# Two fused transformer blocks on one core: products of a constant tile between attention jobs and before norm turns, turns in blocks, new begin times

## The reference

```python
# first block, for each of 2 layers
h = h + 0.5 * swiglu(rmsnorm(h, ffn1_norm[l]), ...)            # 1024 -> 2816 -> 1024
z = rmsnorm(h, mix_norm[l]) @ w_in[l]                          # MLA, differential attention, pooling
...
h = h + merged @ w_out[l]
h = h + 0.5 * swiglu(rmsnorm(h, ffn2_norm[l]), ...)
# after the layers: rmsnorm(h, final_norm)

# second block, for each of 2 layers
x = x + 0.5 * rms_norm(swiglu_2(rms_norm(x, ...), ...), ...)
mix = token_mixing(rms_norm(x, ...), ...)     # windowed GQA with sinks, chunked mLSTM, RWKV-7 scan
x = x + rms_norm(mix, ln_mix_post[l])
x = x + 0.5 * rms_norm(swiglu_2(rms_norm(x, ...), ...), ...)
gate = jax.nn.sigmoid(rms_norm(x, ln_ple_pre[l]) @ w_ple_gate[l])
x = x + rms_norm(gate * (p[l] @ w_ple_proj[l]), ln_ple_post[l])
```

## Time and profile before

| | us |
|---|---|
| median of three runs | 2437.96 |
| lowest, highest | 2436.68, 2438.85 |
| the profiled execution | 2437.84 |
| its span, first to last instruction | 2436.5 |
| PE busy in it | 2380.6 |
| mean granted clock of TensorE | 0.982 |

### The profile page before, as it was taken

One profiled execution on the slowest core, in us unless ns is written; L12 is line 12 of the kernel. 1 busy time (PEld: TensorE's weight loads), 2 busy tenths in 40 slices (PEclk: granted clock), 3 DMA queues, 4 the chain that ended last, 5 costly groups with the idle time before them and its releaser, 6 DMA issues.

```text
span 2436.5 us, 31092 instructions
## 1 busy us (share of the span) xinstructions
PE 2380.6 (98%) x12448; PEld 1932.5 (79%) x12448; DVE 1520.9 (62%) x2296; ACT 1241.0 (51%) x2057; POOL 51.5 (2%) x66
## 2 busy tenths in 40 slices
PE   8999999999999999999999999999999999999998
PEld 6788878888888877888878878778877887877886
DVE  5656786655655778665565576665556558576555
ACT  5455554544544655454454463654455446365445
POOL 0000000000000000000000000000000000000000
PEclk9999999999999999999999999799999999979999
DMA  7555446555555434555555542155545553215563
GB/s 249 183 193 161 122 139 193 182 187 182 182 183 197 151 124 145 185 182 193 187 173 181 192 137 81 47 186 195 189 156 184 188 183 120 89 66 185 181 198 118
DMA packets 110737, 399.95 MB, mean 164 GB/s; under 512 B 12288, under 2 KB 12672, under 8 KB 110336
## 3 DMA queue, kind: packets, MB, share of 16 engines
q1 hardware_dynamic: 110592, 397.96, 49.9%
HBM read 396.86 MB, written 1.05 MB: 163 GB/s over the span
## 4 chain that ended last, share of the span: by engine, by line
PE 92%; DVE 4%; ACT 2%; issue 0%; POOL 0%; DMA 0%; SPq 0%; ACTq 0%
PE ps L489 81%; PE ps L498 4%; DVE wlo L478 1%; PE ps L2050 1%; PE ps L1456 1%; DVE alo L632 1%; PE ps L1420 1%; PE ps L2424 1%; ACT whi L471 0%; ACT ahi L613 0%; PE ps L1411 0%; PE ps L2553 0%; DVE xs L893 0%; PE ps L2542 0%; PE ps L2534 0%
## 5 line engine op out<-in xcount | busy, mean ns | idle before, releaser
L478 DVE TENSOR_TENSOR wlo<-raw,whi 128x1024 fp32r<-128x1024 f32 (+1 forms) x748 | 893.5, 1212 | 250.8 <-ACT whi L471 245.5
L471 ACT CAST whi<-raw 128x1024 fp32r<-128x1024 f32 (+1 forms) x748 | 764.1, 1041 | 295.1 <-PE ps L489 286.2
L489 PE MATMUL ps<-whi,ahi 128*128 128x512 f32 (+2 forms) x2016 | 812.3, 403 | 24.8 <-DVE wlo L478 18.2
L489 PE MATMUL ps<-wlo,ahi 128*128 128x512 f32 (+2 forms) x2016 | 809.4, 401 | 0.0
L489 PE MATMUL ps<-whi,alo 128*128 128x512 f32 (+2 forms) x2016 | 804.5, 399 | 0.0
L489 PEld LDWEIGHTS ps<-whi,ahi 128*128 128x128 f32 x2016 | 380.6, 189 | 124.2 <-DVE wlo L478 32.3
L489 PEld LDWEIGHTS ps<-wlo,ahi 128*128 128x128 f32 x2016 | 381.3, 189 | 82.9 <-issue 1.0
L489 PEld LDWEIGHTS ps<-whi,alo 128*128 128x128 f32 x2016 | 380.8, 189 | 81.1 <-issue 1.4
L489 PE MATMUL ps<-whi,yhi 128*128 128x512 f32 (+1 forms) x948 | 375.6, 396 | 0.5
L489 PE MATMUL ps<-wlo,yhi 128*128 128x512 f32 (+1 forms) x948 | 372.5, 393 | 0.0
L489 PE MATMUL ps<-whi,ylo 128*128 128x512 f32 (+1 forms) x948 | 372.1, 392 | 0.0
(11 more groups left out here) (374 smaller groups left out, 1627.6 us busy)
## 6 DMA issues: line engine op xcount, KB each, us to landing
raw<-stream SPq DMA_DIRECT2D x718, 512.0 KB, 4.1
raw<-stream SPq DMA_DIRECT2D x16, 388.0 KB, 3.1
bcb<-bcs SPq DMA_DIRECT2D x9, 512.0 KB, 4.6
raw<-stream SPq DMA_DIRECT2D x8, 416.0 KB, 3.8
raw<-stream SPq DMA_DIRECT2D x4, 384.0 KB, 3.0
cst<-consts SPq DMA_DIRECT2D x1, 1260.0 KB, 8.1
msc<-misc SPq DMA_DIRECT2D x1, 1160.0 KB, 6.9
xs<-xin SPq DMA_DIRECT2D x2, 512.0 KB, 4.5
```

Source lines behind the costliest of these rows:

```text
L471: act.do.copy(whi[:, n % NSP, 0:w], raw[:, n % NRAW, 0:w]).then_inc(*rounded(n))
L478: dve.do.tensor_tensor(wlo[:, n % NSP, 0:w], raw[:, n % NRAW, 0:w], whi[:, n % NSP, 0:w].bitcast(F), ALU.subtract).then_inc(*rest(n))
L489: m = pe.do.matmul(o, a, b, start=(first and q == 0), stop=(last and q == n - 1))
```

## The change

There are three edits.

First, a new constant tile `warm` (128x128, a copy of the identity in fp32r that DVE makes once) and a helper `rewarm`. It issues on PE as many products as a table `WARM` says for this boundary, lane and step. Each has `warm` as weights and `warm` four times over as 512 columns, is written to a bank that the next step overwrites, and is read by nobody. They stand before the norm turns (`pe_norm`), before scores of jobs (`pe_scores2`, bank 5) and before turns of jobs (`pe_values2`, bank 7). Each of these steps is now split in two: the wait for the bank and the products, then the wait for the data and the work. In `pe_values2` the wait for the copy of the job before stands ahead of the products and the wait for the exponentials behind them. In all there are 77 products: 24 in the jobs of mix2 and 3 in the norm before it, in each of two layers (54), and 23 in other norms.

Second, `turns` is no generator any more: its turns are issued in a row.

Third, every begin time of `PLAN` is new.

```diff
+WARM = {
+    "ffn1_2>mix2": {"pe_norm": (0, 0, 3, 0), "pe_scores2": (0, 0, 0, 0, 0, 2, 0, 5), "pe_values2": (0, 0, 0, 0, 6, 3, 3, 5)},
+    "ffn2>ffn1": {"pe_norm": (0, 0, 2, 0)},
+    "ffn2_2>ple": {"pe_norm": (0, 0, 0, 2)},
+    "final>ffn1_2": {"pe_norm": (0, 3, 3, 0)},
+    "mix2>ffn2_2": {"pe_norm": (0, 0, 0, 1)},
+    "ple>ffn1_2": {"pe_norm": (3, 6, 0, 0)},
+}
...
-        "act_project2": (28.12, 42.6, 53.34, 57.6, 65.86, 80.76, 99.02, 106.66, 111.42, 113.18, 148.8, 152.98),
...
+        "act_project2": (32.16, 37.1, 44.86, 59.1, 67.46, 88.24, 97.82, 103.12, 126.8, 127.96, 146.34, 148.84),
...
+    def rewarm(s, lane, n, bank):
+
+        counts = WARM.get(boundary(s), {}).get(lane, ())
+        for _ in range(counts[n] if n < len(counts) else 0):
+            pe.wait_ge(warm_dve, "made")
+            pe.do.matmul(ps[:, bank, :].rearrange("p (k n) -> p k n", k=4), warm[:, :],
+                         warm[:, :].unsqueeze(1).broadcast_to([128, 4, 128]), start=True, stop=True)
...
-    def turns(t, *each):
-
-        for q, (o, src) in enumerate(each):
-            if q:
-                yield (t + MM * q,)
+    def turns(*each):
+
+        for o, src in each:
             m = pe.do.transpose(o, src, ident)
         return m
...
     def pe_norm(s):
         for i in range(2):
             for hf in range(2):
+                yield turn_time(s, i, hf) - 0.01
+                wait_banks(s, i, hf)
+                rewarm(s, "pe_norm", 2 * i + hf, 2 * i + hf)
                 yield turn_time(s, i, hf)
                 wait_x(pe, s, i, hf)
-                wait_banks(s, i, hf)
...
             dve.wait_ge(load_tab, "pos")
+            if q == 0:
+                dve.do.tensor_copy(warm[:, :], ident).then_inc(*warm_dve("made"))
...
     def pe_scores2(s):
         for n, i, j, t in JOBS2:
-            yield org(s) + 20 + t
+            yield org(s) + 20 + t - 0.01
             k = 128 * (i + 1)
             if n:
                 pe.wait_ge(job_dve, s, n - 1, "mask")
             else:
                 pe.wait_ge(front_act, s, "qT")
                 pe.wait_ge(front_dve, s, "qT", 2)
+            rewarm(s, "pe_scores2", n, 5)
+            yield org(s) + 20 + t
...
     def pe_values2(s):
         for n, i, j, t in JOBS2:
-            yield org(s) + 20 + t + 3.0
+            yield org(s) + 20 + t + 2.99
             k = 128 * (i + 1)
-            pe.wait_ge(job_act, s, n, "exp", 1)
             if n:
                 pe.wait_ge(job_act, s, n - 1, "back")
             else:
                 pe.wait_ge(lstm_dve, s, "mq")
+            rewarm(s, "pe_values2", n, 7)
+            yield org(s) + 20 + t + 3.0
+            pe.wait_ge(job_act, s, n, "exp", 1)
```

More of the change, by code:

```diff
@@ new lines @@
+        "act_latent": (33.58, 34.74, 35.8, 39.26, 39.32, 39.32, 42.82, 49.6, 50.06, 54.44, 55.08, 55.08, 55.08),
+        "act_merged1": (196.34, 200.14, 204.8, 218.18),
+        "act_norm": (18.48, 22.16, 27.8, 28.24),
+        "act_pool1": (115.8, 116.14, 119.48, 132.32),
+        "act_project1": (52.08, 66.06, 85.16, 100.36),
+        "act_square": (17.04, 21.9, 28.32, 28.32),
+        "act_sums1": (151.84, 186.38),
+        "act_turn1": (116.74, 116.74, 190.48, 190.64),
+        "act_turns1": (67.1, 83.14, 100.84),
@@ new lines @@
+        "dve_square": (24.34, 33.08),
+        "dve_state": (131.26, 137.9, 139.52),
+        "dve_sums2": (149.52, 151.34, 172.2, 172.94),
+        "dve_turn2": (173.56, 174.3),
+        "dve_unit0": (55.66, 56.06, 71.02, 84.6, 89.94, 94.94, 108.74, 118.1),
+        "dve_unit1": (67.46, 79.88, 80.6, 86.16, 93.82, 101.66, 124.94, 132.82),
+        "pe_front2": (38.18, 38.8, 42.52, 54.1, 55.84),
+        "pe_group": (138.8, 142.94),
+        "pe_memory": (138.8, 147.52, 154.3, 159.02, 162.74, 168.98, 171.42, 171.42, 172.48, 174.5, 177.7, 178.04,
+            182.76),
@@ L297 @@
[L297 removed]
+        "act_post": (8.86, 9.02, 11.66, 19.76),
+        "dve_post": (5.28, 6.14, 11.66, 16.02, 16.76, 16.76),
+        "pool_post": (7.92, 15.2),
     },
     "ple>ffn1_2": {
[L300 to L305 removed]
@@ L309 @@
+        "pool_post": (-18.08, -0.38),
     },
@@ L377, in program @@
     rope2 = place("rope2", [2, 32])
+    warm = place("warm", [128], R)
     scr = spot[0]
@@ L572, in turn_time, with boundary @@
         return x_ready(s, i, hf) + (1.0 if i and hf else 0.3)
+    def boundary(s):
+        return (PARTS[s - 1][0] if s else "") + ">" + (PARTS[s][0] if s < len(PARTS) else "")
     def timed(s, **lanes):
-        key = (PARTS[s - 1][0] if s else "") + ">" + (PARTS[s][0] if s < len(PARTS) else "")
+        key = boundary(s)
         def one(name, lane):
@@ L773, in pe_hidden @@
                 pe.wait_ge(a_lo, s, 1, 7)
-            m = yield from turns(0, *((ps[:, 3, 256 * k + 128 * i:256 * k + 128 * i + 128],
+            m = turns(*((ps[:, 3, 256 * k + 128 * i:256 * k + 128 * i + 128],
                                        hid[:, (2 * q + i) % 4, 128 * k:128 * k + 128]) for k in range(2) for i in range(2)))
@@ L976, in pe_turn @@
     def pe_turn(sig, s, name, o, bank, b):
-        m = yield from turns(0, *((ps[:, bank, 256 * c + 128 * i:256 * c + 128 * i + 128],
+        m = turns(*((ps[:, bank, 256 * c + 128 * i:256 * c + 128 * i + 128],
                                    o[:, i, 256 * b + 128 * c:256 * b + 128 * c + 128]) for c in range(2) for i in range(2)))
@@ L1034, in pe_chunks @@
                 yield (4 * MM,)
-            m = yield from turns(4 * MM * b, *((ps[:, banks[b], 256 * c + 128 * i:256 * c + 128 * i + 128],
+            m = turns(*((ps[:, banks[b], 256 * c + 128 * i:256 * c + 128 * i + 128],
                                                   src(i)[:, 256 * b + 128 * c:256 * b + 128 * c + 128])
@@ L1202, in pe_latent @@
             pe.wait_ge(front_dve, s, "cn", 1, g)
-            m = yield from turns(4 * MM * g, *((ps[:, 2 + g, 256 * (c % 2) + 128 * i:256 * (c % 2) + 128 * i + 128],
+            m = turns(*((ps[:, 2 + g, 256 * (c % 2) + 128 * i:256 * (c % 2) + 128 * i + 128],
                                                   cn[:, i, 128 * c:128 * c + 128]) for c in cs for i in range(2)))
@@ L1248, in pe_latent @@
                 pe.wait_ge(front_dve, s, "v", 0)
-            m = yield from turns(0, *((ps[0:96, QT_BANKS[b], 256 * (h % 2) + 128 * i:256 * (h % 2) + 128 * i + 128],
+            m = turns(*((ps[0:96, QT_BANKS[b], 256 * (h % 2) + 128 * i:256 * (h % 2) + 128 * i + 128],
                                        qs[:, i, h, :]) for h in ((2 * b, 2 * b + 1) if b < 4 else (8,)) for i in range(2)))
@@ L1437, in pe_values1 @@
                 pe.wait_ge(job_dve, s, n, "mix")
-            m = yield from turns(0, *((ps[:, 7, 128 * j:128 * j + 128], a[:, 128 * j:128 * j + 128])
+            m = turns(*((ps[:, 7, 128 * j:128 * j + 128], a[:, 128 * j:128 * j + 128])
                                       for j in range(2 * (i + 1) if kind == "mla" else i + 1)))
@@ L1588, in pe_turn1 @@
                     pe.wait_ge(*back_turn1(s, 7))
-                yield from pe_turn(job_pe, s, kind, o, bank[b], b)
+                pe_turn(job_pe, s, kind, o, bank[b], b)
     def act_turn1(s, l):
@@ L2384, in pe_rope2 @@
             pe.wait_ge(rec_dve, s, 1, "T")
-            m = yield from turns(0, *((ps[:, 4 + b, 256 * (c % 2) + 128 * i:256 * (c % 2) + 128 * i + 128],
+            m = turns(*((ps[:, 4 + b, 256 * (c % 2) + 128 * i:256 * (c % 2) + 128 * i + 128],
                                        qk2[:, i, 2 * c:2 * c + 2, :].rearrange("p h d -> p (h d)"))
@@ L2413, in pe_values2 @@
                 pe.wait_ge(lstm_dve, s, "mq")
-            m = yield from turns(0, *((ps[:, 7, 128 * q:128 * q + 128], S2[:, n % 2, 128 * q:128 * q + 128])
+            rewarm(s, "pe_values2", n, 7)
+            yield org(s) + 20 + t + 3.0
+            pe.wait_ge(job_act, s, n, "exp", 1)
+            m = turns(*((ps[:, 7, 128 * q:128 * q + 128], S2[:, n % 2, 128 * q:128 * q + 128])
                                       for q in range(2 * (i + 1))))
@@ L2489, in pe_turn2 @@
             pe.wait_ge(job_dve, s, "out", 1)
-            yield from pe_turn(job_pe, s, "att", o_att, 5 + b, b)
+            pe_turn(job_pe, s, "att", o_att, 5 + b, b)
     def act_turn2(s):
@@ L2556, in pe_memory @@
         pe.wait_ge(lstm_dve, s, "out", 1)
-        yield from pe_turn(lstm_pe, s, "mem", hm, 0, 0)
+        pe_turn(lstm_pe, s, "mem", hm, 0, 0)
     def act_memory(s, l):
```

270 lines of the change are left out of this document (125 added, 145 removed), and 61 rows, old and new, of the table PLAN.

## The result

| | before | after |
|---|---|---|
| median of four runs, us | 2438.40 | 2410.51 |
| lowest, highest | 2436.68, 2439.02 | 2409.24, 2412.00 |
| the profiled execution | 2437.84 | 2412.00 |
| its span | 2436.5 | 2410.7 |
| PE busy | 2380.6 | 2363.4 |

The changed kernel takes 0.9887 of the time, 95% interval 0.987 to 0.9904: 27.9 us less, where 16.7 were forecast. The page after, beside the earlier trace rows: busy us of each engine, and the clock in 40 slices.

A forecast was written before the change was run, and what follows sets the result against it. PE, busy 98% of the span, was taken as the bound, with 55.9 us idle and 82 us at half clock. 15.0 + 3.0 - 2.3 + 1.0 = 16.7 us faster gave 2421 us; range 2403 to 2440.

The forecast's parts named there:

- New begin times: Order on all queues at every stage boundary: taken as 0, with 8 us each way in the range.
- Rival two: PE's 25 us of boundary waits for `wlo` and `xs` shrink by half, 12 us: 2409 us, chance 0.11.
- Long stretches: Half-clock pieces late in both mix2 stages run at full clock: 22.3 us gross, 15.0 us net of hops and products.
- DVE-bound piece: Mix2 piece where DVE is nearly full: a quicker PE gains 0, at most 4.6 and 5.6 us in the two layers.
- Rival three: All 82 us at half clock count, DVE-bound pieces shorten too: 41 us less products, 2401 us, chance 0.06.
- The price of the products: 0.23 us each; 19 of 24 in each layer's jobs hidden, the 5 ahead of job 7's turns cost 1.15 us.
- table loads: ACT saves two loads of 1.28 us per mix2 layer: 1 us faster for both layers, between 0 and 5.1.
- short stretches: Brief half-clock windows of 3.4 to 6.8 us: 3 us faster, between 0 and 7.2.
- products elsewhere: Of 29 products outside the jobs, 10 are charged in full: 2.3 us slower, ends 0 and 6.7.
- Rival one: The clock falls later in the jobs but still falls, half of 22.3 us is lost: 2431 us, chance 0.20.
- Rival four: The clock falls where it did, just ahead of 1547 us, and later products only burden PE: 2454 us, chance 0.10.
- Rival five: Long stretches gain, but new begin times add 16 us of waits for `wlo`: 2437 us, chance 0.08.

The follow-up runs named there:

- no_products: The changed kernel without any of its 77 `warm` products, new begin times and turns in a row kept: 2434.08 us, ratio 0.9983.
- old_begin_times: The changed kernel with every begin time of the kernel before, products and turns in a row kept: 2426.95 us, ratio 0.996.
- more_norm: The changed kernel with 17 more products in norms (mix2's norm and final>ffn1_2): 2410.51 us, ratio 0.9891.
- jobs_early: The changed kernel without the last 11 products of each layer, ahead of the turns of jobs 5, 6 and 7: 2425.23 us, ratio 0.9949.
- jobs_late: The changed kernel without the first 13 products of each layer (scores of jobs 5 and 7, turns of job 4): 2432.65 us, ratio 0.9986.

## Why the prediction was right, and where it was off

**New begin times, "I see no reason for either sign and take 0": this is the term that was mis-sized.** Measured: 3.0 us without the products and 16.4 us with them, twice the 8 us that I allowed. My bound of 25 us from the waits would have held, but I weighed the term as if it stood alone. What the pair adds is 9 us of products that the new order lets stand in idle time and 4 to 6 us of clock that falls less often. The order alone takes 5.5 us off the waits for `wlo`, but other waits come up in their place (no_products). I had left out both effects, though the earlier trace rows show a fall behind a stretch that is only partly idle. Rival two had the direction and nearly the time (2409 us), yet not the size of its mechanism: it wanted 12 us off the two waits, and they went from 25.0 to 20.5 us.

**Long stretches.** The forecast was 15.0 us net. What can be read with nothing else moved is old_begin_times. From job 7's mask to the first dense product it took 20.70 us before (1553.99 to 1574.69) and 14.29 (1554.33 to 1568.62): 6.4 us, where my terms without the dense part come to 9.15 - 2.5 - 1.15 = 5.5. In the second layer it is 7.9 us (20.93 to 13.01), where they come to 6.2. The dense part itself, 1.65 us per layer, gave 0.2 (31.72 to 31.50), because there the clock fell once more; it came with the new times. From norm to norm the two mix2 stages took 6.6 and 8.1 us less, 14.6 in both, so this term was right in size.

**The DVE-bound piece at 0** holds. From job 4's scores to job 7's mask it took 16.86 us before (1537.13 to 1553.99) and 17.33 with products and old times (1537.00 to 1554.33). DVE is busy for 16.1 us in both, so it still bounds the piece. How much a quicker PE alone would give isn't shown: 16 products stand in it now (3.6 us) and the clock fell once for 3.4 us. Rival three falls all the same, by its own sign (the piece isn't shorter) and by its time of 2401 us.

**The price of the products.** I called 19 of 24 per layer hidden. At old times none of the 77 is, over the span: PE's own work fell by 28.6 us, its idle time stayed, and the products took 17.5 us back. Some stand in idle time, but idle time comes up again where the quick PE waits. Net it is 11.3 us between the spans, 10.2 between the medians. At new times 9.5 of the 17.5 us are hidden. My sum without table loads was 15.7, too high by 5. As mix2 alone gave 14.6, the fault lies outside it: I had the short stretches at +3.0 us and the products elsewhere at -2.3, and the rest of the kernel took 3.3 us more (14.6 - 11.3), with 3.7 us more of waits for `wlo`. The error in the begin times covered this one. That the two had opposite signs is luck: with 16.4 us for the begin times and the rest as it was, the sum would have said 2405 us.

The Trainium skill (TensorE: Matmul & The Clock Gate, Terms) prices the throttled time at one half. With 82 us of it before and six stretches of 3.4 us in old_begin_times, that gives 31 us. This trace agrees for PE's own work (28.6 us), and not for the time of the kernel, which fell by a third of that, as the products took the rest. The 31 us gross that the prediction sets against the 41 is half of 82 - 20.4; its own terms add up to 22.3 + 7.2 = 29.5.

**Norm products and short stretches.** I forecast 3.0 - 2.3 = 0.7 us; the 29 products are worth 3.7 us at new times. My charge of 0.23 us for each of those in mix2's norm was wrong, as more_norm shows: in the kernel after PE still waits 2.15 us for `xs` behind the three, and six more cost nothing.

**Table loads**, +1 us: 0 within the spread, at old times. **Turns in blocks**, 0: 0.6 us or nothing. **Rival one**: the clock stays at 1.00 in the jobs of the kernel after; it is true of jobs_early. **Rival four**: its turning point was about the right one. It named the 8 products ahead of job 5's scores and job 4's turns; jobs_late leaves out these and the 5 ahead of job 7's scores, and the late ones then run partly at 0.50 and the gain is gone, though even then the kernel isn't slower. The 8 alone weren't tested. **Rival five** falls: `wlo` 12.7 us. The waits for `wlo` did grow, by 3.7 us, but with the products at old times, not with the new ones.

## What to carry to other kernels

Price a new order on the kernel that the other part of the change makes, not on the one you have: an order that leaves idle time where the added work can stand makes that work cheaper, so look for the pair before you add terms up. Products without a reader held TensorE's clock here over stretches of small products. Set them where the engine idles and count each elsewhere at its full 0.23 us; put some ahead of the first idle gap and some where PE becomes the bound. Take PE's own work, the filler and the idle time apart in the page before you believe that something is hidden.
